# Router logits taken from h inside the out-projection, u scaled by GpSimd, and the third expert's weights asked for before the scatter lands

## The chip, the core and the metric

The kernel runs on one core of one Trainium2 chip. The metric is the device time of one execution in microseconds (us); three runs of the kernel before gave 1474.39, 1477.35 and 1476.57, a median of 1476.57. All data is float32.

## What is computed

Two layers (DEPTH = 2) over 512 tokens (256 of context, 256 latent) of 1024 features. A layer normalises and projects the tokens, runs three mixers, projects back (w_out) and adds a mixture of experts. In the second layer only the 256 latent tokens go through the out-projection and the experts. The part that the change touches:

```python
mix = concat([o_da, o_ssd, o_mla]) @ w_out[i]
hx = hx + mod_x[2] * mix[:, n_ctx:]            # hc likewise in layer 0
u_x = ada_norm(hx, norm_ffn_g[i], mod_x[3], mod_x[4])   # rms_norm(h)*g*(1+scale)+shift
def moe_ffn(h, ...):                           # called with u
    aff = sigmoid(h @ router_w)                # 16 experts in 4 groups
    sel = aff + router_bias                    # best group, then its top 2
    for e in range(16):
        he = silu(h @ w_gate[e]) * (h @ w_up[e])
        y = y + gates[..., e:e+1] * (he @ w_down[e])
```

An expert has 6 MB of weights: gate and up of 1024 x 512 and down of 512 x 1024, 2 MB each.

## The kernel before, in words

The program of each engine is written out by hand (one block for each of tensor, vector, scalar, gpsimd and sync), with semaphores between them. Two PSUM banks rotate: open_bank on TensorE waits until the bank before last is read, claim and emptied on VectorE take the results in the same order, read_back makes TensorE wait for a read. h and u lie feature-major: 8 tiles k of 128 features by the tokens.

**Out-projection** (out_projection on TensorE, add_mixed on VectorE). For each of 8 output tiles m there are 8 matmuls (line 768) of 512 columns (256 in layer 1); VectorE adds the gated result into h[m] (L1333), ScalarE squares it (L1582), VectorE sums the squares into rstd (L1015).

**Norm, logits, rows.** TensorE takes the mean over features (norm_mean, L473), VectorE adds EPS (L1023), ScalarE makes the inverse root (rsqrt, L1568 and L1569). VectorE then scales u[k] = h[k]*rstd (L1030), ScalarE applies gain and shift (L1595), TensorE multiplies each u[k] with the router's weights as it comes (router, L778), VectorE copies the 16 rows of logits, TensorE turns them into token-major. to_rows turns u into token rows in two PSUM banks and ScalarE copies them into u_tok (L1697).

**Routing** (router on VectorE, L1387 to L1466). About 40 small operations from the logits to the two chosen experts of each token (chosen_ready, L1426); TensorE counts places with bf16 matmuls (places, L807 to L812), and these stand behind to_rows in its program; VectorE ranks the experts by load, makes the slot of each token (slots_ready, L1447), then the order of experts by rank (order_ready) and the count of passes (passes_ready, L1463).

**Scatter and first rows.** GpSimd, after ut_taken and slots_ready, scatters u_tok into DRAM (slots) with indirect DMAs of 128 rows of 4 KB (L1823): 8 in layer 0 and 4 in layer 1. ScalarE waits for all of them (scattered) and then issues the loads of the first four blocks of 64 rows (L1717), two DMAs of 64 rows of 2 KB for a block. TensorE turns block 0 and block 1 (turn_x) and begins the first gate and up.

**Expert loop.** Experts 0 and 1 are fixed in their places; the others come by rank. A heavy expert has two blocks of 64 tokens, a light one has one: HEAVY = [8, 4], the blocks number 24 in layer 0 and 20 in layer 1. The order of places is 2 blocks, 2 blocks, then light ones and heavy ones mixed. For a block TensorE runs gate and up (L843, 32 instructions), then the down part of the block before (L864). There are three sets of weight buffers (PAIRS = 3); place o uses set o mod 3. SyncE issues the loads (load_gate_up, L1947; load_down, L1952) in a fixed order, and load_gate_up(o) waits until the gates and ups of place o-3 are done, load_down(o) until its down part is done. The set of place 2 is free from the start, but its gate and up buffers hold the router's working tiles until the order is known, and its down buffer is u. The down buffer of place 1 holds u_tok until the scatter has landed. Before the change SyncE waits for order, passes, scattered and x_landed1 in one go (L1965 to L1968), then issues down of place 1 and gate, up and down of place 2.

## Time and profile before

| what | value |
|---|---|
| median of three runs | 1476.57 us |
| profiled execution, its own time | 1477.52 us |
| its span | 1475.7 us |
| TensorE busy | 1216.9 us (82%) |
| VectorE / ScalarE / GpSimd busy | 471.7 / 266.0 / 122.4 us |
| mean granted TensorE clock | 0.894 |
| the chain that ended last | PE 65%, DMA 15%, VectorE 13% |

The profiled execution is 0.95 us above the median. Busy time counts overlapping work on different engines, so the shares don't add up; the chain says what released what. In it the loads of in_exp_w_up account for 11% of the span, the gate and up matmuls for 17%.

### The profile page before, as it was taken

The numbers are of one execution on the slowest core, as the hardware profiler recorded it, in microseconds if no ns is written. First come the engines' busy times: TensorE is split into PE (matmuls) and PEld (weight loads), VectorE is DVE, ScalarE is ACT, GpSimd is POOL, SyncE is SP. The second block draws the span as 40 slices with busy tenths as digits, with TensorE's granted clock in tenths as the row PEclk, the third lists the DMA queues.
The fourth block names the chain that finished last, engine by engine and source line by source line (L and its number), as shares of the span: only waits on it lengthen the run. The fifth ranks groups of instructions, "written<-read, shape, count | busy, mean of one in ns | idle before, by whom it ended". The sixth has DMA issues, their size and how long they took to land.

```text
span 1475.7 us, 13911 instructions
## 1 busy us (share of the span) xinstructions
PE 1216.9 (82%) x5162; PEld 553.8 (38%) x5162; DVE 471.7 (32%) x1088; ACT 266.0 (18%) x564; POOL 122.4 (8%) x107
## 2 busy tenths in 40 slices
PE   4899889888998299999896499967887499787882
PEld 1363333444643133333232246423565133232221
DVE  2311545866713401111010721466563211000014
ACT  1320101224512111111010411101343011010002
POOL 2000033700000200000000100043000100000001
PEclk9899999979999699999999599987599699899995
DMA  9521108649994399999998210032012699999942
GB/s 345 211 105 67 57 0 338 244 191 401 362 366 167 131 358 387 382 383 389 392 423 298 94 57 0 0 107 121 1 58 114 236 378 376 401 400 397 427 168 93
DMA packets 86030, 347.85 MB, mean 236 GB/s; under 512 B 5958, under 2 KB 37387, under 8 KB 63435
## 3 DMA queue, kind: packets, MB, share of 16 engines
q1 hardware_dynamic: 67056, 308.76, 54.2%
q10 hardware_dynamic: 14907, 24.70, 5.0%
q0 software_dynamic: 4000, 13.49, 2.7%
q8 instruction: 42, 0.69, 0.2%
q14 instruction: 25, 0.20, 0.0%
HBM read 302.89 MB, written 44.04 MB: 235 GB/s over the span
## 4 chain that ended last, share of the span: by engine, by line
PE 65%; DMA 15%; DVE 13%; issue 2%; ACT 2%; POOL 1%; ACTq 1%; SPq 0%; POOLq 0%; DVEq 0%
PE ps L843 17%; PE ps L481 11%; DMA ring<-in_exp_w_up 8%; PE ps L864 7%; PE ps L768 6%; PE ps L490 5%; PE ps L424 4%; DMA arena<-in_exp_w_up 3%; DMA ring<-in_w_mod 3%; PE ps L446 2%; PE ps L665 2%; PE ps L747 2%; PE ps L645 1%; PE ps L717 1%; DVE arena L1270 1%
## 5 line engine op out<-in xcount | busy, mean ns | idle before, releaser
L843 PE MATMUL ps<-ring,arena 128*64 128x512 f32 x1024 | 238.7, 621 | 24.1 <-DMA ring<-in_exp_w_up 24.1
L424 PE MATMUL ps<-cst,arena 128*128 128x128 f32 x582 | 104.4, 313 | 89.2 <-DMA arena<-slots 36.8
L481 PE MATMUL ps<-u,ring 128*128 128x512 f32 (+1 forms) x416 | 168.2, 564 | 10.0 <-ACT u L1595 6.2
L1480 DVE TENSOR_TENSOR arena<-arena,ps 128x256 f32<-128x256 f32 x44 | 26.8, 610 | 418.8 <-ACT arena L1730 418.8
L424 PEld LDWEIGHTS ps<-cst,arena 128*128 128x128 f32 x582 | 73.1, 159 | 176.1 <-issue 65.3
L843 PEld LDWEIGHTS ps<-ring,arena 128*64 128x64 f32 x1024 | 73.2, 143 | 167.5 <-issue 141.7
L481 PEld LDWEIGHTS ps<-u,ring 128*128 128x128 f32 x416 | 80.1, 194 | 96.9 <-issue 91.1
L864 PE MATMUL ps<-arena 128*64 128x512 f32 x512 | 115.4, 592 | 0.9 <-ACT arena L1734 0.9
L843 PE MATMUL ps<-arena 128*64 128x512 f32 x384 | 90.4, 626 | 13.6 <-DMA arena<-in_exp_w_up 13.6
L768 PE MATMUL ps<-u,ring 128*128 128x512 f32 (+1 forms) x256 | 83.1, 486 | 1.0 <-DVE u L1324 1.0
L490 PE MATMUL ps<-ring,u 128*128 128x256 f32 (+1 forms) x224 | 76.8, 503 | 7.7 <-DVE arena L1171 7.7
L1730 ACT ACTIVATE arena<-ps 128x256 f32<-128x256 f32 x44 | 16.9, 384 | 339.4 <-PE ps L843 339.4
L446 PE MATMUL ps<-ring,cond 128*32 128x512 f32 x384 | 54.2, 689 | 17.4 <-DMA ring<-in_w_mod 15.7
L1488 DVE COPY arena<-ps 128x512 f32<-128x512 f32 x44 | 30.4, 692 | 110.4 <-PE ps L864 110.4
L864 PEld LDWEIGHTS ps<-arena 128*64 128x64 f32 x512 | 36.4, 137 | 73.5 <-issue 72.1
L768 PEld LDWEIGHTS ps<-u,ring 128*128 128x128 f32 x256 | 48.5, 190 | 34.9 <-issue 30.1
L1830 POOL DMA_INDIRECT arena<-slots,slot_ids x12 | 12.3, 1026 | 588.8 <-ACTq L1766 585.7
L490 PEld LDWEIGHTS ps<-ring,u 128*128 128x128 f32 x224 | 44.4, 200 | 37.7 <-issue 34.4
L1668 ACT ACTIVATE arena<-ps,arena 128x512 f32<-128x512 f32 (+1 forms) x72 | 43.9, 614 | 62.7 <-DVE arena L1271 60.2
L843 PEld LDWEIGHTS ps<-arena 128*64 128x64 f32 x384 | 27.7, 144 | 68.0 <-issue 53.7
L1270 DVE TENSOR_REDUCE arena<-ps 128x2 f32<-128x1024 f32 (+3 forms) x48 | 39.5, 823 | 34.4 <-PE ps L717 27.2
L747 PE MATMUL ps<-arena 128*128 128x64 f32 x320 | 45.9, 287 | 1.9 <-ACT arena L1679 1.9
(269 smaller groups left out, 1179.9 us busy)
## 6 DMA issues: line engine op xcount, KB each, us to landing
ring<-in_w_mod SPq DMA_DIRECT2D x24, 2048.0 KB, 11.1
ring<-in_exp_w_gate SPq DMA_DIRECT2D x22, 2048.0 KB, 22.0
ring<-in_exp_w_up SPq DMA_DIRECT2D x22, 2048.0 KB, 26.9
arena<-in_exp_w_down SPq DMA_DIRECT2D x22, 2048.0 KB, 21.1
slots<-zeros SPq DMA_DIRECT2D x4, 6144.0 KB, 42.5
arena<-in_exp_w_gate SPq DMA_DIRECT2D x10, 2048.0 KB, 21.9
arena<-in_exp_w_up SPq DMA_DIRECT2D x10, 2048.0 KB, 27.7
u<-in_exp_w_down SPq DMA_DIRECT2D x10, 2048.0 KB, 25.1
```

What stands on the lines that cost most here:

```text
L424: return nc.tensor.transpose(dst, src, ident[0:n, 0:n])
L446: last = nc.tensor.matmul(bank[32 * j:32 * j + 32, :], cond[:, k, :], w[:, k2, 512 * j:512 * j + 512], start=(k == 0), stop=(k == 7), tile ...
L481: last = nc.tensor.matmul(bank[row:row + width, 0:T - c0], w[:, k, n:n + width], u[:, k, c0:T], start=(k == 0), stop=(k == KT - 1))
L490: last = nc.tensor.matmul(bank[:, i * width:(i + 1) * width], u[:, k, P * t:P * t + P], w[:, k, n:n + width], start=(k == 0), stop=(k == K ...
L665: last = nc.tensor.matmul(ps[:, 4, 64 * hh:64 * hh + 64], ews[i % 2][d][:, hh, :], xdt_of(i, d)[:, 64 * hh:64 * hh + 64], start=(d == 0 an ...
L747: last = nc.tensor.matmul(ps[:, g % 2, 64 * hh:64 * hh + 64], probs_t[:, n % 2, k, :], v[:, k, 64 * hh:64 * hh + 64], start=(k == 0), stop ...
L768: last = nc.tensor.matmul(bank[:, 0:T - c0], w[:, k, P * m:P * m + P], u[:, k, c0:T], start=(k == 0), stop=(k == KT - 1))
L843: last = nc.tensor.matmul(ps[BLOCK * half:BLOCK * half + BLOCK, 2 + b % 2, :].rearrange("p (s n) -> p s n", s=2), x_k, pair[:, :, a:a + 25 ...
L864: last = nc.tensor.matmul(ps[BLOCK * half:BLOCK * half + BLOCK, 6 + b % 2, :], hid_t[:, f % 2, BLOCK * (f // 2):BLOCK * (f // 2) + BLOCK], ...
L1270: link(v.tensor_reduce(mx[:, s, 0:nm], ps[:, pair:pair + nm, 0:nk], AX.X, ALU.max))
L1488: v.tensor_copy(y_sb[:, b % 2, :], ps[:, 6 + b % 2, :]).then_inc(S("y_ready", l), 1)
L1668: last = a(probs[:, s % 3, m, 0:nk], ps[:, 2 + 2 * (s % 2) + m, 0:nk], ACT.Exp, scale=DA_SCALE if kind == "da" else MLA_SCALE, bias=nb[:, ...
```

## The change

The change does three things.

1. **Logits from h.** logits = rstd * (h @ (gain*rw)) + shift @ rw. VectorE makes gain*rw and the column sums of shift*rw (scale_router) while TensorE runs the first output tiles; TensorE adds one matmul on h[k] for each token kind after each output tile (route), all eight in their own PSUM bank (ROUTER_BANK = 5), the two kinds at column positions 0 and 32. One more matmul spreads the sum of shift*rw (bank shift) and four (two in layer 1) take the mean square per token (token_means). The logits are turned, scaled and shifted, and the routing starts without u. u[k] = h[k]*rstd moves from VectorE to GpSimd; ScalarE's exp for the logits stands ahead of its gain and shift.
2. **Fewer routing operations.** The loops over token tiles (L1397 to L1400, L1412) become single operations. to_rows goes half by half, not tile by tile.
3. **Order of weight loads.** SyncE waits only for order and passes, issues gate and up of place 2, waits for ut_taken, issues its down, then waits for scattered and issues down of place 1.

In TensorE's program, layer 0, after the last output tile, where the prediction's places(l) and to_rows stand. Before (L424 with u is to_rows, L809 the first of places):

```order
L473 MATMUL ps<-rstd,ones_mean 128x512 [waits bank_evacuated,squares_summed]
L778 MATMUL ps<-u,rw 16x512 [waits u_ready,bank_evacuated]
L778 MATMUL ps<-u,rw 16x512 [waits u_ready] x7
L424 MATMUL ps<-cst,rstd 128x16 [waits bank_evacuated]
L424 MATMUL ps<-cst,rstd 128x16 x3
L424 MATMUL ps<-cst,u 128x128 x8
```

and now (L773 is route, L802 token_means, L480 the mean, L431 the turns):

```order
L773 MATMUL ps<-h,arena 16x256 [waits bank_evacuated]
L773 MATMUL ps<-h,arena 16x256
L802 MATMUL ps<-ones_mean,rstd 128x2 [waits bank_evacuated,squares_summed]
L802 MATMUL ps<-ones_mean,rstd 128x2 x3
L480 MATMUL ps<-rstd,ones_mean 128x512 [waits bank_evacuated,squares_summed]
L431 MATMUL ps<-cst,arena 128x16 [waits bank_evacuated,logits_copied]
L431 MATMUL ps<-cst,arena 128x16 x3
L431 MATMUL ps<-cst,u 128x128 [waits u_ready]
```

The logits no longer wait for u; the turns of u still stand ahead of places.

In SyncE's program, layer 0, behind the loads of place 1. Before:

```order
L1969 TENSOR_LOAD passes [waits scattered_0,x_landed1_0,passes_ready,order_ready]
L1970 REGISTER_ALU
L1952 DMA arena<-in_exp_w_down 128x2x2048 [waits down_done_0]
L1973 TENSOR_LOAD order
L1973 ISA x2
L1945 REGISTER_ALU
L1947 ISA [waits gu_done_0]
L1947 DMA arena<-in_exp_w_gate 128x4096
L1947 DMA arena<-in_exp_w_up 128x4096
L1952 DMA u<-in_exp_w_down 128x2x2048 [waits down_done_0]
```

and now:

```order
L2039 TENSOR_LOAD passes [waits passes_ready,order_ready]
L2040 REGISTER_ALU
L2042 TENSOR_LOAD order
L2042 ISA x2
L2017 REGISTER_ALU
L2019 ISA [waits gu_done_0]
L2019 DMA arena<-in_exp_w_gate 128x4096
L2019 DMA arena<-in_exp_w_up 128x4096
L2024 DMA u<-in_exp_w_down 128x2x2048 [waits down_done_0,ut_taken]
L2024 DMA arena<-in_exp_w_down 128x2x2048 [waits down_done_0,scattered_0]
```

Gate and up of place 2 now wait for neither the scatter nor a row load, and down of place 1 stands behind all three loads of place 2.

The diff, cut to its core (left out: the tiles' addresses, ut_count's new order of halves, and semaphores shared by both layers instead of one each):

```diff
             def out_projection(l):
                 c0 = P * FIRST_T[l]
+                def route(k):
+                    read_back(f"mix{l}{k}")
+                    for s in range(c0 // NCTX, 2):
+                        cols = slice(NCTX * s, NCTX * s + NCTX)
+                        last = nc.tensor.matmul(ps[32 * s:32 * s + NE, ROUTER_BANK, cols], rwg[:, s, k, :], h[:, k, cols],
+                                                start=(k == 0), stop=(k == KT - 1), tile_position=(0, 32 * s))
+                    return last
                 pe.wait_ge(S("o_placed"), (units0 * l + len(attention_units(l))) // DA_H)
                 for n in range(2):
                     w = wait_chunk(("out", l, n, 0)).rearrange("p (k n) -> p k n", n=512)
                             last = nc.tensor.matmul(bank[:, 0:T - c0], w[:, k, P * m:P * m + P], u[:, k, c0:T],
                                                     start=(k == 0), stop=(k == KT - 1))
                         close_bank(last)
+                        if name == f"mix{l}1":
+                            pe.wait_ge(S("router_scaled"), l + 1)
+                            bank = open_bank(f"shift{l}")
+                            cols = slice(NE * (c0 // NCTX), 2 * NE)
+                            close_bank(nc.tensor.matmul(bank[:, cols], ones[:, :], shift_sum[:, cols], start=True,
+                                                        stop=True))
+                        if 4 * n + m:
+                            route(4 * n + m - 1)
                     free_chunk(("out", l, n, 0), name)
+                route(KT - 1).then_inc(S("routed"), 1)
+            def token_means(l):
+                pe.wait_ge(S("squares_summed"), NORMS.index(f"{l}ffn") + 1)
+                bank = open_bank(f"mst{l}")
+                for i, t in enumerate(range(FIRST_T[l], TT)):
+                    last = nc.tensor.matmul(bank[:, 2 * i:2 * i + 2], rstd[:, P * t:P * t + P], ones_mean[:, 0:2],
+                                            start=True, stop=True)
+                close_bank(last)
             def router(l):
-                c0 = P * FIRST_T[l]
-                bank = open_bank(f"logits_t{l}")
-                for k in range(KT):
-                    pe.wait_ge(S("u_ready"), ready_base[f"{l}ffn"] + (2 if l == 0 else 1) * (k + 1))
-                    last = nc.tensor.matmul(bank[0:NE, 0:T - c0], rw[:, k, :], u[:, k, c0:T], start=(k == 0),
-                                            stop=(k == KT - 1))
-                close_bank(last)
-                read_back(f"logits_t{l}")
+                pe.wait_ge(S("logits_copied"), l + 1)
                 bank = open_bank(f"logits{l}")
                 for t in range(FIRST_T[l], TT):
-                    last = tr(bank[:, NE * t:NE * t + NE], rstd[0:NE, P * t:P * t + P])
+                    last = tr(bank[:, NE * t:NE * t + NE], logits_row[0:NE, P * t:P * t + P])
                 close_bank(last)
             def to_rows(l):
-                for t in range(FIRST_T[l], TT):
-                    for half in range(2):
+                for half in range(2):
+                    pe.wait_ge(S("u_ready"), ready_base[f"{l}ffn"] + (2 if l == 0 else 1) * (4 * half + 4))
+                    for t in range(FIRST_T[l], TT):
                         n = ut_count(l, t, half)
                         if n >= 2:
                             pe.wait_ge(S("ut_taken"), n - 1)
                         for m in range(4):
-                            last = tr(ps[:, 2 + half, P * m:P * m + P], u[:, 4 * half + m, P * t:P * t + P])
+                            last = tr(ps[:, 2 + n % 2, P * m:P * m + P], u[:, 4 * half + m, P * t:P * t + P])
                         last.then_inc(S("ut_turned"), 1)
...
                 out_projection(l)
                 c0 = P * FIRST_T[l]
+                token_means(l)
                 norm_mean(f"{l}ffn", c0)
                 router(l)
...
             def norm(name, c0):
+                if name in ("0ffn", "1ffn"):
+                    n = (T - c0) // P
+                    bank = claim(f"mst{name[0]}")[:, 0:2 * n].rearrange("p (t c) -> p t c", c=2)
+                    emptied(ts(rstd_tok[:, 0:n], bank[:, :, 0], EPS, None, ALU.add))
                 bank = claim(f"ms{name}")
                 emptied(ts(rstd[:, c0:T], bank[:, 0:T - c0], EPS, None, ALU.add))
                 if name == "0mix":
                     spare(4)
                 dve.wait_ge(S("rstd_ready"), NORMS.index(name) + 1)
-                for k in range(KT):
+                for k in range(0 if name in ("0ffn", "1ffn") else KT):
                     if name == "0mix" and k == 2:
                         spare(1)
                     tt(u[:, k, c0:T], h[:, k, c0:T], rstd[:, c0:T], ALU.mult).then_inc(S("u_scaled"), 1)
...
+            def scale_router(l):
+                dve.wait_ge(S("bcast_landed"), 16 * n_bcast_dmas)
+                dve.wait_ge(S("gain_ready"), 2 * DEPTH)
+                dve.wait_ge(S("mod_placed"), DEPTH * DEPTH_GROUPS)
+                for s in range(FIRST_T[l] // 2, 2):
+                    tt(rwg[:, s], rw[:, :, :], gain[:, l, 1, :, s].unsqueeze(2).to_broadcast([P, KT, NE]), ALU.mult)
+                    link(tt(rws, rw[:, :, :], mod[:, l, 24:32, s].unsqueeze(2).to_broadcast([P, KT, NE]), ALU.mult))
+                    ins = v.tensor_reduce(shift_sum[:, NE * s:NE * s + NE], rws.rearrange("p k e -> p e k"), AX.X, ALU.add)
+                    if s == 0:
+                        link(ins)
+                ins.then_inc(S("router_scaled"), 1)
             def add_mixed(l):
                 c0 = P * FIRST_T[l]
+                scale_router(l)
                 for m in range(KT):
+                    if m == 2:
+                        bank = claim(f"shift{l}")
+                        s0 = c0 // NCTX
+                        emptied(v.tensor_copy(shift_rows[:, s0:2, :],
+                                              bank[:, NE * s0:2 * NE].rearrange("p (s e) -> p s e", e=NE)))
                     bank = claim(f"mix{l}{m}")
...
-                emptied(v.tensor_copy(rstd[0:NE, P * f:T], claim(f"logits_t{l}")[0:NE, 0:T - P * f]))
                 bank = claim(f"logits{l}")[:, 0:TT * NE].rearrange("p (t e) -> p t e", e=NE)[:, f:TT, :]
-                emptied(v.tensor_copy(lg, bank))
+                dve.wait_ge(S("rstd_tok_ready"), l + 1)
+                link(tt(lg, bank, rstd_tok[:, 0:n].unsqueeze(2).to_broadcast([P, n, NE]), ALU.mult))
+                if l == 0:
+                    lg_s, shift_s = lg.rearrange("p (s t) e -> p s t e", t=2), shift_rows.unsqueeze(2).to_broadcast(
+                        [P, 2, 2, NE])
+                else:
+                    lg_s, shift_s = lg, shift_rows[:, 1:2, :].to_broadcast([P, n, NE])
+                emptied(tt(lg_s, lg_s, shift_s, ALU.add))
                 dve.wait_ge(S("logits_exp"), l + 1)
                 link(ts(aff, aff, 1.0, None, ALU.add))
                 link(v.reciprocal(aff, aff))
...
-                for t in range(n):
-                    tt(pr[:, t, :, 0:3], s4[:, t, :, 0:3], s4[:, t, :, 1:4], ALU.add)
-                    tt(pr2[:, t, :, 0:2], s4[:, t, :, 0:2], s4[:, t, :, 2:4], ALU.add)
-                    link(tt(pr[:, t, :, 3:4], s4[:, t, :, 0:1], s4[:, t, :, 3:4], ALU.add))
-                    link(tt(pr[:, t, :, 0:2], pr[:, t, :, 0:2], pr2[:, t, :, 0:2], ALU.max))
+                pr, pr2, s4 = (ap.rearrange("p t g e -> p (t g) e") for ap in (pr, pr2, s4))
+                tt(pr[:, :, 0:3], s4[:, :, 0:3], s4[:, :, 1:4], ALU.add)
+                tt(pr2[:, :, 0:2], s4[:, :, 0:2], s4[:, :, 2:4], ALU.add)
+                link(tt(pr[:, :, 3:4], s4[:, :, 0:1], s4[:, :, 3:4], ALU.add))
+                link(tt(pr[:, :, 0:2], pr[:, :, 0:2], pr2[:, :, 0:2], ALU.max))
...
-                for t in range(n):
-                    last = v.tensor_copy(g4(msk)[:, t], gk[:, t, :].unsqueeze(2).to_broadcast([P, NG, 4]))
-                link(last)
+                link(v.tensor_copy(g4(msk), gk.unsqueeze(3).to_broadcast([P, n, NG, 4])))
...
+                routed = name in ("0ffn", "1ffn")
+                if routed:
+                    l, n = int(name[0]), (T - c0) // P
+                    act.wait_ge(S("routed"), l + 1)
+                    for s in range(c0 // NCTX, 2):
+                        cols = slice(NCTX * s, NCTX * s + NCTX)
+                        last = nc.scalar.copy(logits_row[0:NE, cols], ps[32 * s:32 * s + NE, ROUTER_BANK, cols])
+                    last.then_inc(S("logits_copied"), 1)
+                    wait_evac(f"mst{l}")
+                    rsqrt(rstd_tok[:, 0:n], rstd_tok[:, 0:n], S("rstd_tok_ready"))
                 wait_evac(f"ms{name}")
                 rsqrt(rstd[:, c0:T], rstd[:, c0:T], S("rstd_ready"))
+                if routed:
+                    wait_evac(f"logits{l}")
+                    a(rt[:, 1, FIRST_T[l]:TT, :], rt[:, 0, FIRST_T[l]:TT, :], ACT.Exp,
+                      scale=-1.0).then_inc(S("logits_exp"), 1)
...
-                wait_evac(f"logits{l}")
-                lg, aff = rt[:, 0, f:TT, :], rt[:, 1, f:TT, :]
-                a(aff, lg, ACT.Exp, scale=-1.0).then_inc(S("logits_exp"), 1)
-                for t in range(f, TT):
-                    for half in range(2):
-                        act.wait_ge(S("ut_turned"), ut_count(l, t, half) + 1)
+                for half in range(2):
+                    for t in range(f, TT):
+                        n = ut_count(l, t, half)
+                        act.wait_ge(S("ut_turned"), n + 1)
                         nc.scalar.copy(u_tok[:, t, :].rearrange("p (k q) -> p k q", q=P)[:, :, 64 * half:64 * half + 64],
-                                       ps[:, 2 + half, :].rearrange("p (q k) -> p k q", k=KT)).then_inc(
+                                       ps[:, 2 + n % 2, :].rearrange("p (q k) -> p k q", k=KT)).then_inc(
                             S("ut_taken"), 1)
...
+                cols = slice(P * FIRST_T[l], T)
+                pool.wait_ge(S("rstd_ready"), NORMS.index(f"{l}ffn") + 1)
+                for k in range(KT):
+                    g.tensor_tensor(u[:, k, cols], h[:, k, cols], rstd[:, cols], ALU.mult).then_inc(S("u_scaled"), 1)
                 pool.wait_ge(S("zeros_stored"), 16 * ZERO_DMAS)
                 pool.wait_ge(S("ut_taken"), ut_count(l, TT - 1, 1) + 1)
                 pool.wait_ge(S("slots_ready"), l + 1)
...
                     sp.wait_ge(S("order_ready"), l + 1)
                     sp.wait_ge(S("passes_ready"), l + 1)
-                    sp.wait_ge(S("scattered", l), 32 * (TT - FIRST_T[l]))
-                    sp.wait_ge(S("x_landed1", l), 32)
                     nc.sync.reg_load(passes_left, passes[0:1, l:l + 1])
                     nc.sync.reg_add(passes_left, passes_left, 1)
-                    load_down(1, 1)
                     for o, r in list(enumerate(rank_order(l)))[FIXED:]:
                         e = nc.sync.value_load(order[0:1, r:r + 1], min_val=0, max_val=NE - 1)
                         load_gate_up(o, e)
+                        if o == FIXED:
+                            sp.wait_ge(S("ut_taken"), ut_count(l, TT - 1, 1) + 1)
                         load_down(o, e)
+                        if o == FIXED:
+                            sp.wait_ge(S("scattered", l), 32 * (TT - FIRST_T[l]))
+                            load_down(1, 1)
```

## Rows read from the trace of the kernel before

**Rows 1.** Windows, layer 1's expert loop and a slice of it: us, busy PE PEld DVE ACT POOL, PEclk, DMA, GB/s.
```profile
1165.70:1411.50 245.80, 213.20 (x959) 73.59 (x958) 22.75 (x35) 24.76 (x55) 0.00 (x0) 0.93 1.01 396
1170.00:1216.00 46.00, 44.88 (x216) 15.84 (x214) 4.51 (x7) 5.37 (x12) 0.00 (x0) 0.99 1.02 375
```

**Rows 2.** Timeline, layer 0: out-projection to slots (start, length, engine, line, op).
```profile
410.72 55.20 PE L768 MATMUL ps<-u,ring 128*128 128x512 f32 x128 [0.52 <-DVE u L1324]
473.65 9.02 PE L778 MATMUL ps<-u,rw 128*16 128x512 f32 x16 [4.11 <-ACT u L1595]
472.41 7.97 ACT L1595 ACTIVATE u<-u,mod,gain 128x256 f32<-128x256 f32 x16 [0.82 <-DVE u L1030]
483.44 0.42 PE L424 MATMUL ps<-cst,rstd 16*128 16x16 f32 x4 [0.77 <-DVE rstd L1385]
484.44 0.20 DVE L1389 TENSOR_SCALAR rt<-rt 128x64 f32<-128x64 f32 x1 [0.32 <-ACT rt L1692]
488.47 1.08 ACT L1697 COPY arena<-ps 128x512 f32<-128x512 f32 x2 [0.25 <-PE ps L424]
493.38 0.19 PE L809 MATMUL ps<-arena 128*128 128x16 bf16 x1 [4.44 <-DVE arena L1426]
496.87 0.17 DVE L1447 TENSOR_SCALAR slot_ids<-slot_sum 128x8 int32<-128x8 f32 x1
499.64 0.15 DVE L1463 CAST passes<-small 128x1 int32<-128x1 f32 x1
```

**Rows 3.** Timeline, layer 0: scatter, first row loads, weight loads, first gate and up.
```profile
498.04 1.08 POOL L1823 DMA_INDIRECT slots<-arena,slot_ids  x1 [198.97 <-DVE slot_ids L1447]
511.84 5.33 ACTq L1717 DMA_DIRECT2D arena<-slots  x8
517.28 0.38 SPq L1952 DMA_DIRECT2D arena<-in_exp_w_down  x1
518.55 0.36 SPq L1947 DMA_DIRECT2D arena<-in_exp_w_gate  x1
519.03 8.57 PE L843 MATMUL ps<-ring,arena 128*64 128x512 f32 x32
```

**Rows 4.** The chain that ended last: last scatter of each layer, issue to landing.
```profile
507.13 4.38 DMA slots<-arena,slot_ids
1154.14 4.01 DMA slots<-arena,slot_ids
```

**Rows 5.** Timeline, layer 1: the same places.
```profile
1099.03 27.89 PE L768 MATMUL ps<-u,ring 128*128 128x256 f32 x128 [0.52 <-DVE u L1324]
1149.12 0.17 DVE L1447 TENSOR_SCALAR slot_ids<-slot_sum 128x4 int32<-128x4 f32 x1
1150.21 1.04 POOL L1823 DMA_INDIRECT slots<-arena,slot_ids  x1 [118.08 <-DVE slot_ids L1447]
1165.64 9.53 PE L843 MATMUL ps<-ring,arena 128*64 128x512 f32 x32
1177.09 7.09 PE L843 MATMUL ps<-ring,arena 128*64 128x512 f32 x32
```

**Rows 6.** DMA issues in narrow windows at 511.8, 519.4, 521.3, 1207.3, 1221.4: KB, us to landing.
```profile
arena<-slots ACTq DMA_DIRECT2D x3, 128.0 KB, 2.6
...
arena<-slots ACTq DMA_DIRECT2D x1, 128.0 KB, 7.5
...
arena<-slots ACTq DMA_DIRECT2D x1, 128.0 KB, 16.0
...
ring<-in_exp_w_up SPq DMA_DIRECT2D x1, 2048.0 KB, 17.1
...
arena<-in_exp_w_down SPq DMA_DIRECT2D x1, 2048.0 KB, 10.1
```

**Rows 7.** GpSimd lines: tensor_tensor of 128x512, lowest, median and highest ns.
```profile
L1859 POOL TENSOR_TENSOR arena<-arena x12: 1037/1044/1493, 210.6 to 1022.6; 128x512 f32<-128x512 f32 x12
...
L1871 POOL TENSOR_TENSOR u<-u,rt x12: 1262/1513/1817, 255.9 to 1028.7; 128x512 f32<-128x512 f32 x12
```

More of the change, by code:

```diff
@@ L60 @@
 SCAN_MODS = (1, 1, 1)
+ROUTER_BANK = 5
 MODS_LEFT = 13
@@ L295, in hybrid_dit_kernel @@
         pairs_of = take(NE * NE, late_at + 256).rearrange("p (a b) -> p a b", b=NE)
+        logits_row = take(T, late_at + 1024)
+        rwg = take(2 * KT * NE, late_at + 1536).rearrange("p (s k e) -> p s k e", s=2, e=NE)
+        rws = take(KT * NE, late_at + 1792).rearrange("p (k e) -> p k e", e=NE)
+        shift_sum = take(2 * NE, late_at + 1920)
+        shift_rows = take(2 * NE, late_at + 1952).rearrange("p (s e) -> p s e", e=NE)
+        rstd_tok = take(TT, late_at + 1984)
         vecrows = take(DEPTH * P, 2 * TT * DM).rearrange("p (l n) -> p l n", l=DEPTH)
@@ L359, in ut_count @@
         def ut_count(layer, t, half):
-            return 2 * (TT * layer + t - FIRST_T[layer]) + half
+            return 2 * TT * layer + half * (TT - FIRST_T[layer]) + t - FIRST_T[layer]
         def turned_probs(n, nk):
@@ L672, in scan_tiles @@
                                                     state[r, d, t, :], start=True, stop=True)
-                    last.then_inc(S("y_summed", l), 1)
+                    last.then_inc(S("y_summed"), 1)
                     if i + 1 < len(tiles):
@@ L684, in y_transposes @@
             def y_transposes(l, t, count):
-                pe.wait_ge(S("y_normed", l), count)
+                pe.wait_ge(S("y_normed"), tiles_before(l) + count)
                 bank = open_bank(f"yT{l}{t}")
@@ L1208, in scan_tiles @@
                         clamp(i + 1, 1)
[L1209 removed]
+                    dve.wait_ge(S("y_summed"), tiles_before(l) + i + 1)
                     y_sum = y_sums[i % 2]
@@ L1236, in y_norm @@
                 i = t - FIRST_T[l]
-                dve.wait_ge(S("y_gated", l), i + 1)
-                dve.wait_ge(S("y_squared", l), i + 1)
-                ts(y_sums[i % 2], y_sums[i % 2], small[:, 0:1], None, ALU.mult).then_inc(S("y_normed", l), 1)
+                dve.wait_ge(S("y_gated"), tiles_before(l) + i + 1)
+                dve.wait_ge(S("y_squared"), tiles_before(l) + i + 1)
+                ts(y_sums[i % 2], y_sums[i % 2], small[:, 0:1], None, ALU.mult).then_inc(S("y_normed"), 1)
             def y_turned(l, t):
@@ L1395, in router @@
                 pr2 = w1.rearrange("p t (g e) -> p t g e", g=NG)
-                for t in range(n):
-                    tt(pr[:, t, :, 0:3], s4[:, t, :, 0:3], s4[:, t, :, 1:4], ALU.add)
-                    tt(pr2[:, t, :, 0:2], s4[:, t, :, 0:2], s4[:, t, :, 2:4], ALU.add)
-                    link(tt(pr[:, t, :, 3:4], s4[:, t, :, 0:1], s4[:, t, :, 3:4], ALU.add))
-                    link(tt(pr[:, t, :, 0:2], pr[:, t, :, 0:2], pr2[:, t, :, 0:2], ALU.max))
+                pr, pr2, s4 = (ap.rearrange("p t g e -> p (t g) e") for ap in (pr, pr2, s4))
[3 more added lines that the diff above has]
+                link(tt(pr[:, :, 0:2], pr[:, :, 0:2], pr2[:, :, 0:2], ALU.max))
+                pr = pair.rearrange("p t (g e) -> p t g e", g=NG)
                 gs = w2[:, :, 0:4]
@@ L1648, in scan @@
                         decays(i + 1, 1)
-                    act.wait_ge(S("y_gated", l), i + 1)
+                    act.wait_ge(S("y_gated"), tiles_before(l) + i + 1)
                     link(a(y_two, y_sums[i % 2], ACT.Square, accum_out=small[:, 1:2]))
-                    rsqrt(small[:, 0:1], small[:, 1:2], S("y_squared", l), 1.0 / SSD_INNER, small[:, 20:21])
+                    rsqrt(small[:, 0:1], small[:, 1:2], S("y_squared"), 1.0 / SSD_INNER, small[:, 20:21])
                     if i + 2 < n:
@@ L1888, in _ @@
                 for i in range(len(tiles) - 1):
-                    pool.wait_ge(S("y_summed", l), i + 1)
+                    pool.wait_ge(S("y_summed"), tiles_before(l) + i + 1)
                     x_dt(i + 1, 1)
@@ L1897, in _ @@
                         x_dt(i + 2, 0)
-                    pool.wait_ge(S("y_gated", l), i + 1)
+                    pool.wait_ge(S("y_gated"), tiles_before(l) + i + 1)
                     skip(i + 1)
```

3 lines of the change are left out of this document (1 added, 2 removed).

## Prediction

> **What bounds the kernel now.** I read the windows first: in layer 1's expert loop the DMA engines are full (share 1.01, 396 GB/s over 245.8 us) while TensorE is busy for 213 us of them [rows 1]. Then the timeline of the stretch ahead of each loop, the place the change is in: everything there is one chain, and DMA engines and TensorE both idle in parts of it. In layer 0 the out-projection ends at 465.9, the inverse root at 471.6 (0.82 before ScalarE's gain and shift), these at 480.4, the logits' matmuls at 482.7; VectorE's routing runs from 484.4 to the slots at 497.0, and the passes are known at 499.8 [rows 2]. The scatter starts at 498.0 [rows 3] and its last DMA lands at 511.5 [rows 4]; the first row loads go out at 511.8, the weights of place 2 at 518.5, and the first gate and up starts at 519.0 [rows 3]. Call that start T0. Layer 1: out-projection to 1126.9, slots 1149.3, scatter 1150.2 [rows 5] to 1158.1 [rows 4], T0 1165.6 [rows 5]. Every later weight load waits for TensorE to leave a buffer, so a shift of T0 shifts the loop behind it. The question is what the change does to both T0.
>
> **To the slots.** Removed from the chain in layer 0: the wait for u and the 9.02 us of L778. Added in the out-projection: seven pairs of route matmuls between output tiles. A 512-column instruction takes 55.20/128 = 0.43 us [rows 2], a 256-column one 27.89/128 = 0.22, and the gate and up matmuls, which stand at two column positions as route does, give 32 instructions of 512 columns in 7.09 us, 0.22 each: two positions run side by side [rows 5]. So a pair costs 0.44 us (one after the other 0.88, the upper end), seven 3.1; with the shift matmul and TensorE's wait for the bank of tile 1, which VectorE's read now holds up (0.3 and 0.4, small beside the rest), 3.8 in each layer (layer 1 has one kind, at 0.44 too). scale_router's few operations lie in VectorE's wait for the first tile; without that cover they would cost about 2.
>
> After the last tile, layer 0: the inverse root came at 5.7 us and comes at 6.7, since token_means puts 8 instructions ahead of the mean (four turns of 16 columns took 0.42 us [rows 2]; 0 and 8 x 0.43 = 3.4 are the ends, I take 1 as nearest to the turns; layer 1 has half). Logits are scaled, shifted and through the exp 1.3 us later, so routing starts at 8.0 where it started at 18.5. Choosing took 8.9 and loses about 1.7 with the loops: done at 15. But places stands behind the turns of u, and these wait for GpSimd. Its tensor_tensor of 128x512 took 1.04 to 1.51 us [rows 7]; at 1.1 (separate input and output, as in the first of the two) eight take 8.8, where VectorE was ahead of ScalarE. ScalarE ends gain and shift at 16.7 and then makes eight copies, which took 484.5 to 489.5 [rows 2]: 22. From places to slots it was 3.7 [rows 2]: slots at about 26, against 31.1. With 3.8 in front **the slots come 1.2 us earlier** (4 earlier to 3 later, by the two prices of GpSimd and of route). The wait moved from logits to rows of u. In layer 1, half as wide, choosing (11.5) and rows (11.8) end together, slots at 15.6 after the last tile against 22.4: **3.0 us earlier**.
>
> **Scatter beside weights.** SyncE now asks for place 2 when the passes are known, 2.8 us after the slots, plus its register loads (the second takes 1.27 us from one issue to the next [rows 3]): about 3.5 us after the scatter's start, not 20. What the trace shows of two queues at once: row loads of 128 KB take 2.6 us alone, but issued at 519.4 to 521.3 beside place 2's weights the first landed after 7.5 and the fourth after 16.0 [rows 6], at 526.9 and 537.3: 3.5 us apart. In 3.5 us the engines move 1.3 MB, ten times a row load. That is what alternation piece by piece gives, one row of 2 KB for one weight row of 16 KB: 64 x 18 KB. By the access patterns, a scatter DMA has 128 rows of 4 KB, a gate or up load 128 rows of 16 KB, a down load 256 of 8 KB. So each scatter DMA lets one gate or up load pass, or half a down load. A weight load is 5.6 us at 375 GB/s [rows 1], a scatter DMA 1.3.
>
> Layer 0: the weights begin to move some 5.6 us after the scatter's start, when 2.4 of 8 scatter DMAs are through. The other 5.6 outlast all three loads: 5.6 + 3 x 5.6 + 5.6 x 1.3 = 29.7, landed at 30 us where it was 13.5: **16.5 later**. Down of place 1 then goes out with the first rows; 4 row loads alternate with 256 rows of 8 KB, which adds about **2.5** to the 7.2 between their issue and T0. Layer 1: 1.7 of 4 scatter DMAs are left, each with a gate or up load: 5.5 + 1.7 x 6.9 + 0.3 = 17.5 against 7.9: **9.6 later**. Then the first row loads meet the rest of up, down of place 2 and down of place 1: start 4.4, 2.4 MB of weights 6.4 and the rows 1.4 make 12.2, T0 about 1.1 later, against 7.5: **6 later**. T0 moves by -1.2 + 16.5 + 2.5 = +17.8 and by -3.0 + 9.6 + 6 = +12.6. Unmixed queues are the lower end (0 for all four), the row loads' 17.9 us from first issue to fourth landing [rows 6] the upper for rows.
>
> The Trainium skill, DMA: Bandwidth & Descriptors, section Queues, rings and completion order, says that an engine changes queue only after a whole packet, typically 9 to 17 descriptors. By it each scatter or row DMA would wait for the whole share of a weight load. The trace disagrees: row loads landed 3.5 us apart, not 5.6 + 0.4. By that rule the sum would be about 6 us more.
>
> **What the early weights give back.** 6 MB (17 us) leave the queue behind T0. But the load of place 3 waits for place 0's second block, and later ones likewise. In layer 1 up of place 4, issued at 1207.3, landed after 17.1, at 1224.4; down of place 4, issued at 1221.4, took 10.1 [rows 6]. At 1221.4 three microseconds of up were left, and a load moves nothing in its first 2 to 2.5 us in any case (a row load alone needs 2.6), so the queue was less than a microsecond behind. What lay in it before has no effect after. I take 0.7 per layer; the ends are 0 and 4 (if the queue of then carries what the busy share suggests). The loop's stalls at the end stay, with T0 as origin.
>
> **Sum.** 1477.5 (profiled) + 17.8 + 12.6 - 1.4 = 1506.5; the profiled execution is 0.95 above the median, so 1505.5 against 1476.57.
>
> **Rivals.**
> 1. The scatter keeps its pace since its descriptors are in first, only the row loads are held up. For it: row loads are the only mixed case seen. Against: the same engines serve both queues, and in layer 0 most of the scatter is issued after the weights. Each T0 then moves by the row loads' 17.9 + 1.4 - 7.5 = 11.8, less the slots' gain: 10.6 + 8.8 - 1.4 = +18: **1494.6**.
> 2. Faster. The loop is limited by bytes and not by buffers: with the share at 1.01 [rows 1], work moved into the idle 7 us (511.5 to 519.0, and 1158.1 to 1165.6) comes off the end. It decides if buffers come free early enough that the queue never drains, and the mixing costs only order. Then -1.2 - 7 - 3.0 - 6 = -17: **1459.5**. Against it is the drained queue at 1221.4.
> 3. Whole loads pass between scatter DMAs. 7.5 and 16.0 speak against it [rows 6]: **1511.5**.
> 4. The change doesn't do what it says: slots no earlier (GpSimd at 1.51 us adds 3.3 and 1.6) and the loads land without touching the scatter, since they go out late: **1476.5**, no change.
>
> **How the numbers follow.** Forecast 0.50 (own range 1498 to 1514), rival 1 0.26, rival 2 0.15, rival 3 0.05, rival 4 0.04. The range 1476 to 1514 takes in all but rival 2 and some of the tails. A measurement tells about 0.2% (3 us) from no change. Faster is rival 2 and a little of rival 4, 0.16; same 0.04; slower 0.80.
>
> **What the profile will show.** Right: L778 gone, passes known within 3 us of before, gate of place 2 issued about 20 us earlier; GpSimd's scatter landings far above 4.4 us; the first gate and up 12 to 18 us later in both layers; DMA engines idle for some 16 us after it. Wrong: scatter landings near 4 us (rival 1 or 2); the DMA share near 1 all through the first 20 us of the loop, or the last waits for in_exp_w_up gone (rival 2); slots more than 5 us earlier, which would mean that GpSimd or the row copies cost less than I take.

## The result and the profile after

The changed kernel takes **1520.74 us**, median of four runs (1513.93 to 1523.44), against 1476.96 for the kernel before, four runs beside it. The ratio is 1.0279, 95% interval 1.0247 to 1.0311: slower by 2.8%. The profiled execution of the changed kernel took 1513.93 us, the fastest of its four, with a span of 1512.1 us (before 1475.7) and a mean granted TensorE clock of 0.880 (before 0.894). TensorE's busy time is nearly the same, 1217.2 us (before 1216.9): what was added is waiting.

Timeline of the changed kernel, layer 0, from the scaling of u to the first gate and up; columns as in [rows 2, 3]. L1889 is GpSimd's scaling of u, L1438 and L1444 make the logits, L1482 ends choosing, L836 is the first matmul of places, L1785 loads the rows:

```profile
478.86 9.88 POOL L1889 TENSOR_TENSOR u<-h,rstd 128x512 f32<-128x512 f32 x8 [179.34 <-ACT rstd L1625]
480.17 0.21 DVE L1438 TENSOR_TENSOR rt<-ps,arena 128x64 f32<-128x64 f32 x1
480.42 1.05 DVE L1444 TENSOR_TENSOR rt<-rt,arena 128x64 f32<-128x64 f32 x1
481.66 8.20 ACT L1665 ACTIVATE u<-u,mod,gain 128x256 f32<-128x256 f32 x16
483.95 1.17 DVE L1454 TENSOR_TENSOR rt<-rt 128x48 f32<-128x48 f32 x1
...
493.94 0.22 DVE L1482 TENSOR_TENSOR arena<-rt 128x64 bf16<-128x64 f32 x1
495.62 0.17 PE L836 MATMUL ps<-arena 128*128 128x16 bf16 x1
498.85 0.17 DVE L1503 TENSOR_SCALAR slot_ids<-slot_sum 128x8 int32<-128x8 f32 x1
500.01 1.08 POOL L1895 DMA_INDIRECT slots<-arena,slot_ids  x1 [11.28 <-DVE slot_ids L1503]
...
504.04 0.20 SPq L2019 DMA_DIRECT2D arena<-in_exp_w_gate  x1
529.07 0.38 SPq L2024 DMA_DIRECT2D arena<-in_exp_w_down  x1
529.39 5.35 ACTq L1785 DMA_DIRECT2D arena<-slots  x8
538.83 1.12 PE L431 MATMUL ps<-cst,arena 128*128 128x128 f32 x4 [42.70 <-DMA arena<-slots]
541.74 1.12 PE L870 MATMUL ps<-ring,arena 128*64 128x512 f32 x2
```

The gate of place 2 goes out at 504.04, 14.5 us earlier than in [rows 3]. The scatter starts 2.0 us later, at 500.01, and the row loads go out at 529.39: 29.4 us after its start, where it was 13.8. TensorE sits idle for 42.7 us. The first gate and up (T0) starts at 541.74, 22.7 us later than in [rows 3].

Layer 1, the same view, and two rows of the chain that ended last (issue, us to landing), which answer to [rows 4] and [rows 5]:

```profile
1169.02 0.17 DVE L1503 TENSOR_SCALAR slot_ids<-slot_sum 128x4 int32<-128x4 f32 x1
...
1189.17 5.31 ACTq L1785 DMA_DIRECT2D arena<-slots  x8
1203.45 2.83 PE L870 MATMUL ps<-ring,arena 128*64 128x512 f32 x6
```

```profile
509.11 19.94 DMA slots<-arena,slot_ids
1174.04 14.81 DMA slots<-arena,slot_ids
```

The last scatter DMA takes 19.94 us from issue to landing where it took 4.38, and in layer 1 14.81 where it took 4.01. Layer 1's T0 is 37.8 us later than in [rows 5], and the end 36.4.

What the DMA engines do after T0, windows with the columns of [rows 1]:

```profile
541.70:560.00 18.30, 17.18 (x71) 5.71 (x72) 0.60 (x1) 1.93 (x4) 0.00 (x0) 0.87 0.14 44
1203.50:1221.00 17.50, 16.38 (x67) 5.43 (x68) 0.60 (x1) 1.93 (x4) 0.00 (x0) 0.85 0.15 46
1203.50:1449.00 245.50, 212.72 (x959) 73.54 (x958) 22.75 (x35) 24.76 (x55) 0.00 (x0) 0.93 0.92 363
```

The weights that went ahead leave the DMA engines nearly idle for 18 us behind each T0 (shares of 0.14 and 0.15), and the loop takes as long as before: 245.5 us at a share of 0.92, where [rows 1] have 245.8 at 1.01.

### The profile page after: what moved, and what is told of

It is laid out like the page before. It is cut to its first block, busy times and chain, and to the rows that moved or that the text cites. A ratio compares the mean times of both kernels' runs of the same rounds, so it can differ in the third digit from the quotient of the medians.

```text
span 1512.1 us, 13986 instructions
## 1 busy us (share of the span) xinstructions
PE 1217.2 (80%) x5194; PEld 555.7 (37%) x5194; DVE 474.6 (31%) x1065; ACT 268.5 (18%) x571; POOL 137.6 (9%) x123
## 4 chain that ended last, share of the span: by engine, by line
PE 63%; DMA 18%; DVE 13%; issue 2%; ACT 2%; POOL 1%; SPq 0%; ACTq 0%; POOLq 0%; DVEq 0%
PE ps L870 17%; PE ps L488 11%; DMA ring<-in_exp_w_up 8%; PE ps L891 7%; PE ps L784 6%; PE ps L497 5%; PE ps L431 4%; DMA arena<-in_exp_w_up 3%; DMA ring<-in_w_mod 3%; PE ps L453 2%; DMA slots<-arena,slot_ids 2%; PE ps L672 2%; PE ps L754 2%; PE ps L652 1%; DMA arena<-slots 1%
## 5 line engine op out<-in xcount | busy, mean ns | idle before, releaser
L431 PE MATMUL ps<-cst,arena 128*128 128x128 f32 (+1 forms) x588 | 104.6, 310 | 129.7 <-DMA arena<-slots 77.9
L431 PEld LDWEIGHTS ps<-cst,arena 128*128 128x128 f32 (+1 forms) x588 | 73.0, 158 | 217.8 <-DMA arena<-slots 75.1
L1902 POOL DMA_INDIRECT arena<-slots,slot_ids x12 | 12.2, 1020 | 627.9 <-ACTq L1834 624.8
```

Of the source, the lines that this page charges most:

```text
L431: return nc.tensor.transpose(dst, src, ident[0:n, 0:n])
```

## Experiments

Each ran beside the kernel before; a ratio is to that, with its 95% interval. Experiments 1 to 4 ran on one chip and 5 to 8 on another. The kernel before had a wider spread there (1474.97 to 1488.98 us, median 1479.6, on the first; 1475.26 to 1492.72, median 1479.5, on the second), so ratios are what to compare. "Scatter" is the time from the first scatter's start to the issue of the first row loads, "rows" the time from there to T0; for the kernel before they are 13.8 and 7.2 us in layer 0, 8.3 and 7.2 in layer 1.

**1. The new logits alone.** SyncE's old order in the changed kernel:

```diff
+                    sp.wait_ge(S("scattered", l), 32 * (TT - FIRST_T[l]))
+                    sp.wait_ge(S("x_landed1", l), 32)
+                    load_down(1, 1)
                     for o, r in list(enumerate(rank_order(l)))[FIXED:]:
                         load_gate_up(o, e)
-                        if o == FIXED:
-                            sp.wait_ge(S("ut_taken"), ut_count(l, TT - 1, 1) + 1)
                         load_down(o, e)
-                        if o == FIXED:
-                            sp.wait_ge(S("scattered", l), 32 * (TT - FIRST_T[l]))
-                            load_down(1, 1)
```

> The new logits, GpSimd's scaling and the new order of turns, but SyncE asks for the third expert's weights where it did before, behind the landed scatter and the first rows. Theory A (the whole loss is weight loads passing among the scatter's and the row loads' pieces): scatter landings as before (last one 13.5 us after the first scatter starts in layer 0, 7.9 in layer 1), rows to first gate and up 7.5 us in both, so the first gate and up comes later only by what the new front shows in the changed kernel, about +2.0 us in layer 0 and +0.2 in layer 1: 1476 to 1481 us. Theory B (the new front itself, by a slower GpSimd, a lower clock or the memory it uses, makes what follows slow): above 1490. Theory C (the front does gain, and only the scatter hides it): below 1473.

Measured: 1.0016 (0.999 to 1.0041), span 1477.5. The scatter takes 13.9 us in layer 0 (500.14 to the row loads at 514.05) and 9.2 in layer 1, where its last DMA took 4.96 us instead of 4.01 with no weights beside it; the rows take 7.2 and 7.5. T0 is 2.2 and 0.8 us later than before. Theory A holds, B and C fall: the new front gains nothing, and what it costs is within the interval.

**2. The early weights alone.** The mirror image: the kernel before with the lines above taken out and put in.

> The kernel before with SyncE's new order alone: place 2's gate and up asked for when the passes are known, its down behind the last row copy, down of place 1 behind the scatter. Theory A: scatter 29 us in layer 0 and 18 to 19 in layer 1, rows +5 and +7, less 3.0 and 1.4 given back later: about +34, a profiled run of 1511 and a median of 1508 to 1520. Theory B: 1474 to 1480, since the old front is back. If the first weights meet the scatter at another phase because the old front ends 2 us earlier, the landing may lie up to 6 us off either way.

Measured: 1.0239 (1.0197 to 1.028), span 1509.8, 34.1 us over the profiled run of before. T0 is 20.9 and 36.3 us later. The scatter takes 29.2 us to the row loads in layer 0 and 18.8 in layer 1. So about 34 of the 36.4 us (by the ratios, 2.4 of the 2.8%) come from the order of SyncE's loads alone.

**3. Rows beside weights, scatter not.** The changed kernel with place 2 held until the scatter has landed:

```diff
+                    sp.wait_ge(S("scattered", l), 32 * (TT - FIRST_T[l]))
                     for o, r in list(enumerate(rank_order(l)))[FIXED:]:
```

> As the changed kernel, but place 2's gate goes out only when the scatter has landed, together with the first row loads and ahead of down of place 1. Theory A with one alternation law for every load: scatter 13.5 and 7.9 us as before; each of the first four row loads then alternates with rows of 16 KB, 64 x 18 KB or 3.1 us each, so the first gate and up starts 12 to 16 us after the scatter landed in both layers instead of 7.5: 1490 to 1503. If only the scatter suffers from weights beside it: 1476 to 1482. If weights pass before any row load: above 1505.

Measured: 1.0127 (1.0084 to 1.017), span 1494.0. The scatter is back at 13.9 and 9.5 us. The rows take 15.3 and 15.2 us to T0, 8 more than before, in both layers, inside the range expected. Both scatter and rows pay when weights run beside them, each for what it moves.

**4. The changed kernel again.**

> The changed kernel again, for a second profile. Its four runs lay between 1513.9 and 1523.4 where those of before lay within 3.5 us; the profiled one was the fastest. Theory A1 (the spread is the phase in which weights and scatter meet): the profile of a run near 1520 has the scatter's landing or the first gate and up 3 to 8 us later than 29.0, 12.7, 18.7 and 14.6 us, and the loops as long as in the first profile. Theory A2 (the spread is in the loops): landings within 1 us of those, and one or both loops longer by the difference.

Measured: 1.028 (1.0234 to 1.0326), four runs of 1515.9 to 1524.3; profiled 1521.02, span 1519.2. The scatter takes 29.3 and 19.8 us, the rows 12.9 and 14.4, about as in the first profile (29.4, 12.4, 19.1, 14.3). The loops aren't what differs most either: from T0 to the start of layer 1's projections it is 325.6 us in both profiles. What differs most is layer 1's mixer, from there to the out-projection, 255.6 us against 251.4, a stretch that the change doesn't touch. Windows of it in before, in the changed kernel's first profile and in this one:

```profile
843.60:1099.00 255.40, 221.91 (x806) 126.67 (x806) 122.90 (x265) 58.30 (x125) 32.00 (x24) 0.85 0.11 42
```
```profile
867.30:1118.70 251.40, 218.62 (x806) 125.34 (x806) 122.95 (x266) 58.38 (x125) 31.91 (x24) 0.86 0.11 42
```
```profile
865.50:1121.10 255.60, 222.57 (x806) 127.68 (x806) 122.96 (x266) 58.32 (x125) 32.07 (x24) 0.85 0.11 42
```

The same 806 matmuls keep TensorE busy for 3.3 us longer in before and for 4.0 us longer in this profile than in the changed kernel's first one, at a lower granted clock. The last 240 of them show it best: 49.8 us at a granted clock of 0.81 in before, 47.8 at 0.84 in the first profile, 49.9 at 0.81 in this one. Over the ten profiles of this case the mixer takes either 251.4 to 252.2 us (the changed kernel's first, experiments 1, 2 and 6) or 254.1 to 255.6 (before and the others), whatever the kernel. So the changed kernel's first profile was 4 us lucky against before. Neither A1 nor A2 is right: 4.2 of the 7.1 us between the two profiles lie in this stretch, the rest in pieces of 2.2 us and less. What decides between the two lengths is open.

**5. Smaller rows in the weights of place 2.** Each of its gate and up loads becomes two (left out: the loads of the other places stay whole, and TensorE's wait counts the additional landings):

```diff
+                            for c in range(2):
+                                quarter = "p i (a c n) -> p c (i a) n"
+                                sp.dma_start(dst.rearrange(quarter, a=2, c=2)[:, c],
+                                             src.rearrange(quarter, a=2, c=2)[:, c]).then_inc(
+                                                 S(f"gu_landed{o % PAIRS}", l), 16)
```

> The changed kernel, with gate and up of place 2 each loaded by two DMAs whose rows are 4 KB (every second 4 KB of the old 16 KB rows); bytes, order and waits are the same. Theory A (the two queues take turns row by row): a scatter DMA of 128 rows of 4 KB then lets 0.5 MB pass and not 2 MB. Layer 0: 5.6 scatter DMAs let 2.9 of the 4 MB of gate and up pass, 8 us, so the scatter lands some 20 to 23 us after its start and not 29; layer 1: 1.7 scatter DMAs let 0.9 MB pass, 10.5 to 13 us and not 18.7. The rows behind it still meet the rest of up and both down loads: 8 to 13 us to first gate and up. Together 10 to 20 us less than the changed kernel, a ratio to before of 1.014 to 1.021. Theory D (the engines finish what stands ahead in whole loads, or share time by bytes): landings as in the changed kernel within 2 us, ratio 1.025 to 1.031.

Measured: 1.0237 (1.0189 to 1.0284), span 1510.0. The scatter takes 24.6 and 14.6 us to the row loads, 4.8 and 4.5 less than in the changed kernel; the rows 14.5 and 14.9, 2.2 and 0.6 more. Both landings moved far beyond the 2 us of theory D, but neither into the range of theory A (20 to 23 and 10.5 to 13 us), and the rows took longer than the 8 to 13 us expected; the ratio lies between the two theories. Why so little was gained is in the queues' rows. Packets (a packet here is one row), MB and share of 16 engines in windows of 3 us: the changed kernel beside gate and up (from 509.01) and beside a down load (from 518.01); then this kernel in the first mixed 3 us (from 504.25) and nine later (from 513.25). q0 is the scatter's queue, q1 that of the weights.

```profile
q1 hardware_dynamic: 65, 1.06, 86.6%
q0 software_dynamic: 54, 0.19, 15.7%
...
q1 hardware_dynamic: 108, 0.78, 61.8%
q0 software_dynamic: 108, 0.39, 32.0%
```
```profile
q1 hardware_dynamic: 173, 0.71, 90.6%
q0 software_dynamic: 19, 0.01, 2.3%
...
q0 software_dynamic: 172, 0.63, 51.4%
q1 hardware_dynamic: 169, 0.63, 51.0%
```

The counts of packets are equal, or nearly, whatever a packet holds: 65 to 54 with rows of 16 KB beside 4 KB, 108 to 108 with 8 KB, 169 to 172 with 4 KB. The bytes are then 5.6, 2 and 1 to one. Equal counts alone would also fit turns of several rows each, but the single records of the trace don't: beside gate and up in the changed kernel, from 506 to 512 us, 94% of the scatter's rows end within 10 ns of the start of a weight row, where 20% would do so by chance, and only 10% within 10 ns of the next scatter row; here, from 510 to 520 us, it is 98% and 22%, where 50% would by chance. So an engine takes turns a row at a time. The third pair is where this does not hold: for some 3 us behind the start of the weights, the scatter got 19 packets against 173. My expectation left that out.

**6 and 7. VectorE scales u.** Both have SyncE's old order of loads, as experiment 1. GpSimd's scaling goes to VectorE, behind the shift of the logits; VectorE's wait for the inverse root, which stood ahead of the logits, moves to it. Experiment 6 also issues places(0) ahead of the turns of the last three token tiles of u:

```diff
                 emptied(tt(lg_s, lg_s, shift_s, ALU.add))
+                dve.wait_ge(S("rstd_ready"), NORMS.index(f"{l}ffn") + 1)
+                for k in range(KT):
+                    tt(u[:, k, cols], h[:, k, cols], rstd[:, cols], ALU.mult).then_inc(S("u_scaled"), 1)
...
+                        if (l, half, t) == (0, 1, 1):
+                            places(l)
```

> The new logits with the old order of weights (as in the first experiment), VectorE scaling u itself after it has shifted the logits, without its wait for the inverse root ahead of them, and in layer 0 the matmuls of places ahead of the last three turns of u. The trace of the changed kernel shows VectorE's first two-input operations at 0.64 to 1.30 us where the like took 0.16 to 0.17 before, exactly while GpSimd scales. Theory F (GpSimd and VectorE hold each other up): these fall to 0.2 us, choosing ends 3 us earlier in layer 0 and 1.2 in layer 1, slots 4.5 and 1.2 us earlier than in the first experiment, the ratio to before 0.996 to 0.999. Theory G (these operations are slow by their shape): they stay at 0.6 to 1.3 us, and the ratio is 1.000 to 1.003.

> As the kernel before this in the list, but the matmuls of places stay behind all turns of u. Theory F: slots 2.2 us earlier than in the first experiment in layer 0, where the turns bind, and 1.2 in layer 1; ratio to before 0.998 to 1.001. Theory G: no later and no earlier than the first experiment by more than 1 us.

Measured: experiment 6 0.9968 (0.9945 to 0.9991), span 1468.0; experiment 7 0.999 (0.9966 to 1.0014), span 1474.4. From the start of the out-projection to the slots it is 83.2 us in layer 0 in experiment 6 (408.46 to 491.66) and 84.1 in experiment 7, against 87.7 in experiment 1; in layer 1 48.7 in both, against 50.3. Experiment 7's gain of 3.6 us in layer 0 are more than the 2.2 expected; the early places of experiment 6 are worth only the other 0.9. Timeline of experiment 6, VectorE:

```profile
475.26 0.22 DVE L1449 TENSOR_TENSOR rt<-rt,arena 128x64 f32<-128x64 f32 x1
476.18 4.91 DVE L1453 TENSOR_TENSOR u<-h,rstd 128x512 f32<-128x512 f32 x8 [0.70 <-ACT rstd L1634]
...
482.07 0.21 DVE L1463 TENSOR_TENSOR rt<-rt 128x48 f32<-128x48 f32 x1
```

The operation of 128x48 that took 1.17 us while GpSimd scaled takes 0.21, the addition of the shift 0.22 where it took 1.05, at the same shapes. Theory F holds for VectorE, which GpSimd holds up; that VectorE slows GpSimd no run shows. G falls. The gain of the two kernels is not this effect alone: VectorE also makes the eight multiplications in 4.91 us where GpSimd took 9.88. Experiment 6 is 0.3% faster than the kernel before, experiment 7 can't be told from it.

**8. Gate of place 2 alone, early.** Does the loop give anything back for 2 MB that are there ahead of time?

```diff
-                        load_gate_up(o, e)
-                        if o == FIXED:
-                            sp.wait_ge(S("ut_taken"), ut_count(l, TT - 1, 1) + 1)
-                        load_down(o, e)
+                        load_gate_up(o, e, (0,) if o == FIXED else (0, 1))
                         if o == FIXED:
                             sp.wait_ge(S("scattered", l), 32 * (TT - FIRST_T[l]))
+                            sp.wait_ge(S("x_landed1", l), 32)
                             load_down(1, 1)
+                            load_gate_up(o, e, (1,))
+                        load_down(o, e)
```

> The new logits with only the gate of place 2 asked for when the passes are known; down of place 1, up and down of place 2 go out where they did before. Theory A with alternation row by row: the scatter lasts 5.6 us longer in layer 0 (19 us) and 4.5 to 5.6 in layer 1 (13), the rows 7.5 us as before. What the loop gives back decides the time: if the loop is held by its buffers, nothing, and the ratio to before is 1.007 to 1.011; if it is held by bytes, the 2 MB that are ahead come off its end, 5.5 us per layer, and the ratio is 0.999 to 1.003.

Measured: 1.0076 (1.0048 to 1.0104), span 1490.5. The scatter takes 19.6 and 14.3 us, the rows 7.2 and 7.5 as before. From layer 0's T0 to layer 1's out-projection it is 579.7 us, where before had 580.0, and from layer 1's T0 to the end 311.5, where before had 310.1. From T0 to the start of layer 1's projections, without the mixer, it is 324.6 us in both. So the loop gives nothing back for bytes that are ahead, which is what a loop held by its buffers does.

## Why the prediction was wrong

The direction, the mechanism and the place were right; the time, 1505.5, and the range up to 1514 were too low. T0 was to come 12 to 18 us later in each layer; counted from the start of the out-projection it came 22.2 and 18.1 us later. On the profiled runs the sum was 29.0 us over before, and 36.4 were measured. By its terms, each read from the starts in the two traces:

| term | predicted | measured |
|---|---|---|
| layer 0: up to the out-projection | 0 | +0.5 |
| layer 0: out-projection to slots | -1.2 | +1.5 |
| layer 0: scatter | +16.5 | +15.6 |
| layer 0: rows to T0 | +2.5 | +5.2 |
| T0 to layer 1's out-projection | -0.7 | -3.0 |
| layer 1: out-projection to slots | -3.0 | +0.2 |
| layer 1: scatter | +9.6 | +10.8 |
| layer 1: rows to T0 | +6 | +7.1 |
| T0 to the end | -0.7 | -1.4 |

**Scatter beside weights** was the step with the large price, and it holds: 26.4 us for 26.1 (0.9 too much in layer 0 and 1.2 too little in layer 1, so that so close a sum is partly luck). Row by row is what the queues show, and experiment 2 carries nearly the whole loss. Rival 1 (rows alone are held) falls with experiments 2 and 3; rival 2 (faster) with the share of 0.14 behind T0 and with experiment 8; rival 4 with the scatter. Rival 3, whole loads between scatter DMAs, would have come nearer to the time, 1511.5, but by the wrong mechanism: the Trainium skill, DMA: Bandwidth & Descriptors, section Queues, rings and completion order, says that an engine drains a whole packet of typically 9 to 17 descriptors before it changes queue. The single records disagree where both queues have been running for a while (experiment 5: one row, then one of the other queue); the 3 us at the start of its weights, in which the scatter got 19 packets against 173, look like it, but no run here shows what they are.

**"The slots come 1.2 us earlier"** and **"3.0 us earlier"** are the step that failed: +1.5 and +0.2, so 5.9 us in all. Its parts are all in the trace. A route pair takes 0.61 us and not 0.44, and with the other additions layer 0's out-projection is 4.9 us longer instead of 3.8. GpSimd's multiplication takes 9.88/8 = 1.23 us each and not 1.1, and ScalarE begins only at 481.66, since in its program the Exp of the logits stands ahead of the gain and waits for VectorE; ScalarE ends 18.5 us after the last tile instead of 16.7. And GpSimd holds VectorE up. I took choosing to last 7.2 us in layer 0 (8.9 less 1.7); from L1446 at 481.79 to L1482 at 493.94 it is 12.2, and 6.9 in experiment 6, where GpSimd is idle. In layer 0 the turns of u hid that, in layer 1 choosing ends last and it shows: 8.4 us there, 6.0 in experiment 6. Experiments 6 and 7, which take GpSimd out, get back 3.6 to 4.5 and 1.6 us. The Trainium skill has the rule: SBUF — State Buffer, section SBUF: two separate sides, says that VectorE and GpSimd share one pair of ports as an exclusive lock, taken among others by a VectorE operation with two SBUF inputs. The trace agrees: L1438, whose one input is in PSUM, took 0.21 us in the midst of it, L1444 with both in SBUF 1.05. It also shows operations with one input held up: the cast in L1434 took 1.29 us for 0.22 in experiment 6, the addition of a constant in L1446 0.87 for 0.19, but the reciprocal behind it kept its 0.55. I had costed what GpSimd takes, and not what it does to the engine beside it.

**"Which adds about 2.5"** to layer 0's rows was +5.2. The row loads were costed as taking turns with the down load from their start. In the two windows behind their issue, of 4 us and of 2 us, the queues moved this (q10 is that of the rows):

```profile
q1 hardware_dynamic: 129, 1.06, 76.2%
...
q1 hardware_dynamic: 78, 0.64, 83.4%
q10 hardware_dynamic: 59, 0.12, 16.6%
```

In the first 4 us no row moved at all; before, 77 row packets had moved within 2 us of issue. The weights of the down load, issued 0.3 us ahead of the rows, had the engines to themselves. Layer 1 has the same: none of its rows moved in the 4 us behind 1189.17. It looks like the 3 us of experiment 5, but that it is the same is not shown. The trace of before had it too: of the rows issued from 519.39 on, none moved until 523.14. The prediction took the spacing of those landings, 3.5 us, and left out what stood ahead of the first. Layer 1's +7.1 for 6 is near.

**"What the early weights give back"** was right in kind. The -3.0 in front of layer 1's out-projection is not given back by the loop: T0 to layer 1's projections is 1.0 us *longer* than before, and the -4.0 behind it is the mixer, for the most part its granted clock (experiment 4). The -1.4 at the end is no more than what profiles differ by there (307.9 to 311.5 us over the ten). One reading behind this term was off: a load does not stay still for 2 to 2.5 us, its first row moved 1.3 us after issue (row loads issued at 511.84, first row at 513.19). Without the mixer's -4.0 the sum is +40, and the median, 43.8 over before, is near. The profiled run, those 4 us included, was the fastest of four and 6.8 us under their median, which is the second half of the miss: I took the relation of profile to median from before, 0.95 us above, as fixed, and the range had no term for it.

## What to carry to other kernels

When a chain of small-row DMAs is on the critical path, price what runs beside it by rows and not by bytes: each of its rows lets one row of the other queue pass, so 16 KB weight rows beside 4 KB rows leave it a fifth or less of the engines (15.7% here). Weights asked for earlier are worth something only if the loop behind is short of bytes; look at whether the load after them waits for a buffer before you move them. And work given to GpSimd is not free for VectorE: look for VectorE operations on SBUF in the same stretch, those with two inputs above all, however short.

## Hardware behaviour that I had not expected

- In layer 0, VectorE operations with both inputs in SBUF took 0.63 to 1.30 us beside GpSimd's multiplications, against 0.18 to 0.23 in experiment 6 without them; a cast and an addition of a constant, with one input, took 1.29 and 0.87 against 0.22 and 0.19; one with an input in PSUM kept its 0.21.
- For 3 to 4 us after a second queue starts, one of the two can get next to nothing, and not always the one that came last. In the changed kernel the row loads, behind the weights, moved no row for 4 us in either layer. In experiment 5 it was the queue already running that got 19 packets against 173 for 3 us.
- Layer 1's mixer takes 251.4 to 252.2 or 254.1 to 255.6 us, from profile to profile and whatever the kernel, with its last 240 matmuls at a granted clock of 0.84 or 0.81. In the run lists the time falls as the mean clock rises: the kernel before at 0.896 took 1475, at 0.884 1489.
